# A two-layer hybrid block with one attention block: modulation tiles loaded in the second pair, two weight pieces of the first pair in other places, the last copy ahead of squares

## The reference

```python
h2 = rmsnorm(x, norm_mlp)
x = x + jnp.square(jax.nn.relu(h2 @ w_up)) @ w_down
...
jnp.split(jax.nn.silu(cond) @ w_mod + b_mod, N_MOD, axis=-1)
```

## Time and profile before

| | |
|---|---|
| time, median of 3 runs | 2466.93 us (2464.65 to 2468.66) |
| the profiled execution's own time | 2464.23 us |
| its span, first to last instruction | 2462.4 us |
| TensorE busy | 2431.9 us, 12088 matmuls |
| VectorE, ScalarE, GpSimd busy | 1370.5, 953.0, 1346.8 us |
| DMA | 247.75 MB, mean 101 GB/s |
| five fast groups begin at | 605, 696, 786, 1470, 1560 us |

### The profile page before, as it was taken

How to read it: one execution, slowest core, us unless ns; L and a number is a source line. 1 busy time by engine, 2 the same in 40 slices (tenths; PEclk the granted TensorE clock), 3 DMA queues, 4 the chain that set the end, 5 groups by cost and what they waited for, 6 DMA issues and landing times.

```text
span 2462.4 us, 34600 instructions
## 1 busy us (share of the span) xinstructions
PE 2431.9 (99%) x12088; PEld 2022.9 (82%) x12088; DVE 1370.5 (56%) x1957; ACT 953.0 (39%) x1363; POOL 1346.8 (55%) x1652
## 2 busy tenths in 40 slices
PE   9999999999999999999999999999999999999999
PEld 7888888888888888888888888888777777888887
DVE  7884412367676768944123665637876665633333
ACT  5332232242443523312322424424577775422222
POOL 6556655556556665566555565566432324555554
PEclk9999999999999999999999999999999999999999
DMA  5223222343333332122232323343211112232322
GB/s 195 79 69 102 94 95 95 100 145 116 116 137 137 112 103 86 65 98 94 95 101 94 145 100 141 120 166 108 84 42 49 59 41 69 95 102 85 103 93 94
DMA packets 64909, 247.75 MB, mean 101 GB/s; under 512 B 7200, under 2 KB 9888, under 8 KB 63520
## 3 DMA queue, kind: packets, MB, share of 16 engines
q1 hardware_dynamic: 62496, 218.13, 26.5%
q10 hardware_dynamic: 2304, 28.17, 2.9%
HBM read 244.17 MB, written 2.10 MB: 100 GB/s over the span
## 4 chain that ended last, share of the span: by engine, by line
PE 87%; DVE 4%; ACT 3%; DMA 2%; issue 2%; DVEq 1%; POOL 1%; SPq 0%; ACTq 0%; POOLq 0%
PE ps L702 82%; DMA w_raw<-weights 2%; PE ps L1078 1%; PE ps L1091 1%; PE ps L1107 1%; DVE ps L2272 1%; ACT set_hi L1406 1%; PE ps L1046 1%; ACT A_hi L1439 1%; DVE E L2299 1%; POOL w_lo L601 1%; DVEq L2266 1%; DVE set_lo L2279 0%; ACT prob L1710 0%; PE ps L1111 0%
## 5 line engine op out<-in xcount | busy, mean ns | idle before, releaser
L601 POOL TENSOR_TENSOR w_lo<-w_raw,w_hi 128x256 fp32r<-128x256 f32 x1448 | 1176.9, 846 | 883.8 <-ACT w_hi L1327 646.3
L702 PE MATMUL ps<-H_hi,w_hi 128*128 128x512 f32 x1616 | 641.9, 397 | 0.2 <-DVE H_lo L2469 0.2
L702 PE MATMUL ps<-H_hi,w_lo 128*128 128x512 f32 x1616 | 629.5, 390 | 0.0
L702 PE MATMUL ps<-H_lo,w_hi 128*128 128x512 f32 x1616 | 629.2, 389 | 0.0
L1327 ACT ACTIVATE w_hi<-w_raw 128x1024 fp32r<-128x1024 f32 x295 | 310.2, 1054 | 481.7 <-PE ps L702 480.8
L702 PEld LDWEIGHTS ps<-H_hi,w_hi 128*128 128x128 f32 x1616 | 303.4, 188 | 69.4 <-issue 9.1
L702 PEld LDWEIGHTS ps<-H_lo,w_hi 128*128 128x128 f32 x1616 | 303.5, 188 | 64.9 <-issue 4.5
L702 PEld LDWEIGHTS ps<-H_hi,w_lo 128*128 128x128 f32 x1616 | 303.4, 188 | 63.9
L702 PE MATMUL ps<-A_lo,w_hi 128*128 128x512 f32 x744 | 289.6, 389 | 0.0
L702 PE MATMUL ps<-A_hi,w_hi 128*128 128x512 f32 x688 | 267.7, 389 | 0.0
L702 PE MATMUL ps<-A_hi,w_lo 128*128 128x512 f32 x688 | 267.7, 389 | 0.0
(11 more groups left out here) (331 smaller groups left out, 4016.2 us busy)
## 6 DMA issues: line engine op xcount, KB each, us to landing
w_raw<-weights SPq DMA_DIRECT2D x403, 512.0 KB, 3.3
mod_w<-mod_weights ACTq DMA_DIRECT2D x8, 3072.0 KB, 10.7
toeplitz<-biases SPq DMA_DIRECT2D x14, 128.0 KB, 2.2
out<-X SPq DMA_DIRECT2D x7, 256.0 KB, 2.0
X<-x SPq DMA_DIRECT2D x3, 512.0 KB, 7.5
decay_sb<-decay ACTq DMA_DIRECT2D x1, 1024.0 KB, 6.2
ctx_sb<-context ACTq DMA_DIRECT2D x1, 1024.0 KB, 14.6
X<-x SPq DMA_DIRECT2D x2, 256.0 KB, 4.3
```

What stands on the lines that cost most here:

```text
L601: last = nc.gpsimd.tensor_tensor(lo[:, c:c + LOW_COLS], w_raw[:, q, c:c + LOW_COLS], hi[:, c:c + LOW_COLS].bitcast(F32), ALU.subtract)
L702: mm = nc.tensor.matmul(dst, w[l], xs[r], start=start and a == 0, stop=stop and a == 2, skip_group_check=joined)
```

## The change

Five edits. The modulation tiles of a fast group are requested by ScalarE in pair 1 (j = 1), behind `keep_second`, instead of ahead of the group; other groups are as before. A22 lies at place 5 instead of 7, and S4 of odd pairs at 7 instead of 5. S1 of a group's first pair is summed in E[:, 0] instead of in its own place of `set_lo`; VectorE sums it behind down block 6 instead of 7, and waits for E's last readers instead of for the place; ScalarE's high half waits for the place instead. In the first pair, A22's high half stands ahead of S1's. In the last pair, `keep_second` stands ahead of the high half of the next down block and of the squares.

```diff
--- before.py
+++ after.py
@@ -139,7 +139,7 @@
 T1, T2, T3, T4 = range(4)
 
 PIECES = ("A11", "S3", "S2", "S4", "A12", "S1", "A22")
-PLACE = {"A11": 0, "S3": 1, "S2": 2, "S4": 3, "A12": 4, "S1": 6, "A22": 7}
+PLACE = {"A11": 0, "S3": 1, "S2": 2, "S4": 3, "A12": 4, "S1": 6, "A22": 5}
 READY_ORDER = (1, 0, 3, 2, 5, 4, 7, 6)
 MASKED = 1e30
 BIG = 3e38
@@ -483,7 +483,7 @@
 
         def place(piece, pair):
 
-            return PLACE[piece] + (2 * (pair % 2) if piece == "S4" else 0)
+            return PLACE[piece] + (4 * (pair % 2) if piece == "S4" else 0)
 
         def raw_of(piece, n):
 
@@ -492,6 +492,8 @@
 
         def sum_place(piece, n):
 
+            if FAST_JOBS[n][2] == 0 and piece == "S1":
+                return E[:, 0, :]
             if FAST_JOBS[n][2] == 0:
                 return set_lo_f[:, place(piece, PAIR_OF[n]), :]
             return ps[:, SUM_OF_BANK[piece], :]
@@ -1400,7 +1402,7 @@
                     whole = raw_of(piece, n)
                 else:
                     act.wait_ge(piece_summed[piece], i + 1)
-                    if FAST_JOBS[n][2]:
+                    if FAST_JOBS[n][2] or piece == "S1":
                         free_of(act, piece, n)
                     whole = sum_place(piece, n)
                 high = nc.scalar.activation(set_hi[:, s, :], whole, ACT.Copy)
@@ -1448,7 +1450,12 @@
                     act.wait_ge(piece_used["S3"], PAIR_OF[last_pair] + 1)
                 nc.scalar.activation(w_hi[:, s, :], w_raw[:, s, :], ACT.Copy).then_inc(w_hi_ready, 1)
 
-            def fast_up(n0):
+            def load_mod(L, g):
+
+                act.wait_ge(mod_used, L * FF_GROUPS + g + 1)
+                act.dma_start(mod_w[:, :, :], mod_weights[L * FF_GROUPS + g]).then_inc(mod_loaded, 16)
+
+            def fast_up(L, g, n0):
 
                 for j in range(DT // 2):
                     n = n0 + 2 * j
@@ -1464,10 +1471,14 @@
                     if j:
                         piece_highs("A22", n)
                     if not more:
+                        keep_second(n)
                         block_high(n0 + DT, n)
                     if j:
                         squares_of(n - 2, 1)
-                    keep_second(n)
+                    if more:
+                        keep_second(n)
+                    if j == 1:
+                        load_mod(L, g)
                     if more:
                         piece_highs("S2", n + 2)
                         piece_highs("S4", n + 2)
@@ -1490,8 +1501,8 @@
                     for piece in (("A11", "S3"), ("S2", "S4"), ("A12",))[m - 5]:
                         piece_highs(piece, first)
                     if m == DT - 1:
+                        piece_highs("A22", first)
                         piece_highs("S1", first)
-                        piece_highs("A22", first)
                 else:
                     block_high(n0 + m + 3)
 
@@ -1628,10 +1639,10 @@
                 for g in range(FF_GROUPS):
                     rg = r + (JOB_FF + g * FF_GROUP_JOBS) // RING
 
-                    act.wait_ge(mod_used, L * FF_GROUPS + g + 1)
-                    act.dma_start(mod_w[:, :, :], mod_weights[L * FF_GROUPS + g]).then_inc(mod_loaded, 16)
+                    if (L, g) not in FAST:
+                        load_mod(L, g)
                     if (L, g) in FAST:
-                        fast_up(rg * RING)
+                        fast_up(L, g, rg * RING)
                     elif g == 0:
                         norm_round(rg, 2 * L + 1)
                         scaled_halves(L)
@@ -2264,7 +2275,10 @@
                         for b in range(n, n + 2):
                             dve.wait_ge(w_loaded[b % RING], (b // RING + 1) * 16)
                     fence()
-                    if FAST_JOBS[n][2] == 0:
+                    if FAST_JOBS[n][2] == 0 and piece == "S1":
+                        if i:
+                            dve.wait_ge(e_squared, 2 * i)
+                    elif FAST_JOBS[n][2] == 0:
                         free_of(dve, piece, n)
                     a, b, op = {"S3": (a11, a21, ALU.subtract), "S2": (a22, sum_place("S3", n), ALU.subtract),
                                 "S4": (a12, sum_place("S2", n), ALU.subtract),
@@ -2355,8 +2369,9 @@
                         sum_of("S2", n)
                         sum_of("S4", n)
                         sum_low("S3", n)
+                    elif m == 6:
+                        sum_of("S1", n)
                     elif m == 7:
-                        sum_of("S1", n)
                         sum_low("S1", n)
 
                 def mod_step(g, k):
```

## The result

The changed kernel takes 2472.93 us (median of 17 runs) beside 2464.82 us for the kernel before (17 runs): a ratio of 1.0029, 95% interval 1.0021 to 1.0036, so 8.1 us slower. One of the 17 runs of the changed kernel took 3449.89 us at a mean granted clock of 0.65 and is not in the ratio. The forecast was 2476.5 us, 9.6 us above a kernel before of 2466.9. The profiled executions differ by 9.0 us (2473.26 to 2464.23).

A forecast was written before the change was run, and what follows sets the result against it. TensorE bounds the kernel, busy in all but some 30 us of 2462.4. Idle terms lose 10.0 us together, the clock gives -0.4: +9.6 on a median of 2466.9, so 2476.5 us; eight in ten from 2461 to 2487.

The forecast's parts named there:

- The collision moved and grew: Pair 3's weights meet the modulation load moved to pair 1 and land six us too late for VectorE; chance 0.54.
- Both strands: From A22 of pair 0 to the modulation load (via `kept`) and to pair 3's weight loads (via GpSimd), within 1 us.
- Idle before S1 of pair 2: TensorE idle 4.8 us per group behind the late weights of pair 3, 24.0 us lost in five groups.
- Bank waits: TensorE's waits for VectorE to free a bank: 3.4 us become 4.9, 1.5 lost.
- Clock: TensorE's clock dips at idle of 5 us in none to five groups: -3.4 to +1.6 us; with three, -0.4.
- clock falls in all groups: Rival: TensorE idle 5.5 us per group, landing after 13.4 us, clock low in every group: 2482 to 2486 us; chance 0.12.
- Part 1: A22 at place 5, S1 summed in E: pair 2's loads go 3.3 us earlier, unopposed; idle before pair 1's S1 gains 10.8.
- Part 3: `kept` ahead of block high and squares in the last pair: 0.76 us idle before its S1 goes, 3.7 us gained.
- The rule of the skill: Each DMA engine drains a whole packet, some 9 to 17 descriptors, before the next queue; by it the time would be 2446.

The follow-up runs named there:

- only_mod_moved: The kernel before with one edit, the modulation load moved to pair 1 behind `keep_second`: 2480.86 us, ratio 1.0062 to the kernel before.
- mod_pair2: The changed kernel with the modulation load one pair later, in pair 2 behind its first copy: 2441.41 us, ratio 0.9899 to the kernel before.
- pieces_4k: The changed kernel with modulation tiles stored so that an element of the load is 4 KB, not 24 KB: 2465.78 us, ratio 1.0001 to the kernel before.
- mod_ahead: The changed kernel with the modulation load back ahead of each fast group: 2455.80 us, ratio 0.9956 to the kernel before.
- mod_small: The changed kernel with only one of six modulation tiles loaded in fast groups: 2442.53 us, ratio 0.9906 to the kernel before.

## Why the prediction was right, and where it was not

*The collision moved and grew.* Right. Both strands hang on A22 of pair 0, and pair 3's weights went out 1.2 us behind the modulation load in all five groups; the forecast was within 1 us. Forecast, from the group's start: landing at +26.8, S1 of pair 2 at +30.9. Measured in group (0,2): +27.0 and +31.0. That close a match is partly luck: the modulation load went out at +13.6, half a microsecond earlier than forecast, and the second block landed 13.4 us after it instead of 12.7. In the five groups this time is 12.4 to 13.7 us, 12.9 on average. VectorE's wait for weights: forecast 25 to 32 us in 5 times, measured 26.5. That it is this collision, and nothing in the other edits, `only_mod_moved` and `mod_pair2` show from both sides.

*Idle before S1 of pair 2.* Forecast 24.0 us in five groups, measured 20.8 (3.5 to 4.8 in each). *Bank waits.* Forecast 4.9, measured none. *Clock.* Forecast -0.4 with a dip in three groups; measured some 8 us more than before, since it fell in all five and in four of them stayed down longer than in the kernel before, where a dip cost 1.7 us. The two last terms were mis-sized against each other: I let a dip take 0.7 us of the bank wait, and it took all. The waits for `kept` and the bank together grew by 2.9 us and TensorE's busy time by 6, where I had 10.0 and -0.4; the total is near because the misses cancel. The rival "clock falls in all groups" came true in its mechanism, and not in its size: it had 5.5 us of idle time and 2482 to 2486 us (its terms give 2484 at most).

*Part 1, "nothing of this is on TensorE's path by itself".* Wrong. TensorE had no wait in pair 0, but VectorE, once no load is late, hands pair 0's bank back 1 us after TensorE wants it, and the edits of part 1 remove just that: 5.9 us. The sum had this gain in it unnamed, since it let pair 2's bank wait vanish. *Part 3.* The mechanism is right; 3.7 us forecast, 5.1 measured without a collision, of which 3.8 are the wait itself. With the collision there is less to gain: `only_mod_moved` shows 1.5 us of this wait in all.

*The rule of the skill.* With pieces of equal size the turns are one for one; with 24 KB against 4 KB the small ones got 0.25 of 2.17 MB. The rule of the Trainium skill (DMA: Bandwidth & Descriptors, "Queues, rings and completion order") that a ring's whole packet of several descriptors goes in one turn would, as the prediction worked it out, have let the weights through; the traces do not agree.

So the change holds two useful parts, worth 5.1 us (part 3) and 5.9 us (part 1) when no load is late, and one placement that costs more than they gain. With the load one pair later, or on SP behind the weights, the kernel takes 2441.4 us.

## To carry to other kernels

A large prefetch is best placed where it is issued just after the small urgent loads of the same stage, and the time that it takes to land (3 MB, 10.7 us at the median of the eight in the kernel before) must fit before the next ones are wanted. Look for this window in the landing times; to move such a load by one iteration is not yet to hide it. Where two engines issue both, their order is left to the race of two strands; one queue makes it sure. A wait that stands in no list can still be one step behind a larger one: value an edit in a kernel from which the larger wait has been taken.

## What the runs showed of the hardware

- A DMA that stands behind an instruction in ScalarE's program may go out ahead of its execution: the modulation load was issued at 711.23, with `kept`, in front of it in the program, starting at 712.20. It went out 0.09 us after the first of two squares had started, the last instruction in front of it for which the trace shows a wait. It is so in all five groups, and in `only_mod_moved` too. The forecast had put it behind `kept`.
- A weight load issued 1.2 us behind the modulation load gave no data for some 3.5 to 4 us, with pieces of 24 KB (the changed kernel) or 4 KB (`pieces_4k`) in front; after that the engines took turns piece by piece. Issued 0.08 us behind it (`mod_ahead`) it gave none for 2.0 to 2.5 us, and 1.2 us behind a load of 512 KB (`mod_small`) for about 1, hardly longer than alone. What sets this lead was not tried.
- After idle times of 3.5 to 4.8 us the clock was at its lower level in every group of the changed kernel: in four it fell while TensorE stood idle, in group (1,1) 0.3 us after it had started again. The length of the pause alone does not decide: in `pieces_4k` the clock stayed up through and behind a pause of 3.32 us and fell at pauses of 2.52 and 2.57.
- A fall of the clock can hide a short wait behind it: TensorE's wait of 0.97 us for the bank is missing at that place in the groups in which it ran at half speed just before.
